# Leaving out the matmuls whose results nobody reads, in a two-block transformer kernel on one core

## The chip, the cores and the metric

One Trainium2 chip, one of its cores. TensorE (PE) multiplies, VectorE (DVE) and ScalarE (ACT) do the elementwise work and empty PSUM, GpSimd (POOL) has a small part, and SyncE (SP) issues most of the DMAs. The metric is the device time in microseconds of one execution, the median over the runs. Lower is better.

## What is computed

The reference runs one sequence of 512 latent tokens and 256 context tokens, width 1024, float32, through three layers. The first has windowed attention with 16 query heads and 4 key heads and a learned sink; a block of 128 latent queries sees its neighbour blocks and all 256 context keys, a context block sees the context alone:

```python
    q_lat, k_lat, v_lat = project(h_lat)
    q_ctx, k_ctx, v_ctx = project(h_ctx)
    ...
        s_lat = jnp.einsum('bqhgd,bkhd->bhgqk', q, k).astype(jnp.float32)
        s_lat = jnp.where(ok, s_lat, NEG_INF)
        s_ctx = jnp.einsum('bqhgd,bkhd->bhgqk', q, k_ctx).astype(jnp.float32)
        p = softmax_with_sink(jnp.concatenate([s_lat, s_ctx], axis=-1), sink_g).astype(v.dtype)
```

The second layer has a gated linear scan (4 heads, both directions, chunks of 64 tokens), of which only the 512 latent rows go on:

```python
        A = jnp.where(lower, jnp.einsum('bqhd,bkhd->bhqk', q_dec, k_inv), 0.0)
        o = jnp.einsum('bhqk,bkhv->bqhv', A, vc) + jnp.einsum('bqhd,bhdv->bqhv', q_dec, S)
        ...
        S = jnp.exp(b_last)[..., None] * S + jnp.einsum('bkhd,bkhv->bhdv', k_end, vc)
```

Each has a multilayer perceptron behind it. The third layer has another attention, a state space model and a mixture of 16 experts. The result is x, 512 by 1024.

## The kernel before, in words

All engines run their own straight program, written by hand in `backbone_kernel`, and meet at semaphores; nothing reorders it. Weights come as tiles of 128 by 1024 on one queue into a ring of 4 (`RAW`), and ScalarE and VectorE split each into a high and a low part (`WH`, `WL`), so that a float32 product becomes three matmuls (`three`, L396 to L398).

**First attention.** The list `heads_of_blocks` gives 96 steps `aa`: 4 key heads g, in each 6 blocks b of 128 queries (0 to 3 latent, 4 and 5 context), in each 4 query heads hh. A step handles 128 queries against 512 keys (b of 0 and 3), 640 keys (b of 1 and 2) or 256 keys (b of 4 and 5). TensorE's part of one step is, in this order: the transposes of the step's exponentials (`transposes`, L734; each transpose is two records in the trace); then `keep_clock`; then the scores two steps ahead (`scores`, L715 to L722 against latent keys, L396 to L398 against context keys); then the weighted values of the step before (`weighted_values`, L745 to L749). At hh of 1 the output of the block before is turned (`out_turned`, L758). ScalarE takes the exponentials (L1177) and the high parts of the transposes (L1186), VectorE the low parts (L1685), the row maxima (L1671, L1675), the scaling of a block's outputs (L1693 to L1706) and, in 64 of the steps, one piece of a modulation product (`mod_stream`, L456).

**Gated scan.** For each of 4 heads h: two tiles of projections, two gate products, a token-major projection of the values (`token_tiles`), then `keep_clock`, then for each direction d the key transposes (`key_transposes`, L844) and `scan`. `scan` alternates per pair of chunks the mixing matrix (L859), the state updates (`updates`, L873, on 64 rows) and, for the four latent pairs, `output` (L889 and L893), which calls `keep_clock` after its waits. Behind a head come two tiles of the output gate (L396 to L398).

`keep_clock` (L447) issues n plain matmuls of 512 columns on 128 rows, with weights and data taken from `HH`, into a PSUM stretch that the following work overwrites with its own first matmul. It has no wait of its own and signals nobody. Its three counts are set at L312:

```python
            for _ in range(n):
                pe.matmul(out, HH[:, KT - 1, 0:P], HH[:, KT - 1, P:P + 512], start=True, stop=True)
```

Of the kernel before, what the change touches and what calls it, by code (L numbers as in the profile page):

```python
# [182 lines left out]
def backbone_kernel(nc, a, out_d):  # L183
# [3 lines left out]
    with ctx:  # L187
# [121 lines left out]
        TWO_PI = 6.283185  # L309
        SSM_PREP = 28  # L310

        STEP_FILL, SCAN_FILL, HEAD_FILL = 1, 2, 12  # L312
        MN = TQ
        SCAN_TILES = [[4, 5, 0, 1, 2, 3], [5, 4, 3, 2, 1, 0]]

# [2070 lines left out]
```

## Time and profile before

| | us |
|---|---|
| median of 3 runs | 3479.77 |
| the three runs | 3477.26, 3479.77, 3495.88 |
| span of the profiled execution | 3475.3 |
| lowest run minus that span | 2.0 |
| mean granted TensorE clock over the span | 0.891 of full |
| first attention, from its first transpose to its end | 216.4 to 586 |
| the four key heads of it begin at | 216.4, 303.1, 411.4, 504.9 |
| gated scan, four heads | 1361.6 to 1749 |

The profile lists only the span of the profiled execution, from its first to its last instruction; its own time in the way of the runs isn't given apart, so the lowest run stands beside it. Busy time, the granted clock and the waits are read from that one execution. In the clock column 1.00 is the upper of TensorE's two levels (2.4 GHz) and 0.50 the lower (1.2 GHz); a value between is a mean over a stretch that has both.

### The profile page before, as it was taken

Reading aid. Unit: us, or ns where it says so; the run is one execution under the profiler, and the core shown is the slowest. Engines: PE = TensorE matmul, PEld = TensorE weight load, DVE = VectorE, ACT = ScalarE, POOL = GpSimd, SP = SyncE. Lnnn points to the kernel's source line nnn. Section 1 sums busy time; section 2 is a strip of 40 time slices with the busy share of each in tenths; the row PEclk is TensorE's granted clock in tenths of the full one; section 3 lists DMA queues with packets and bytes.
Section 4 is the critical chain, followed back from the end, with each engine's and each line's share of the span. In section 5 each row is a group of like instructions: output and inputs, shape, how many; then the busy total and the mean of one; then the engine's idle time right before and its main releaser. Section 6 shows DMA issues by size and latency. Waiting matters only on the chain.

```text
span 3475.3 us, 38477 instructions
## 1 busy us (share of the span) xinstructions
PE 3052.2 (88%) x14418; PEld 2523.9 (73%) x14418; DVE 1751.9 (50%) x2824; ACT 1081.9 (31%) x1673; POOL 172.2 (5%) x151
## 2 busy tenths in 40 slices
PE   1999999879999979888987999887767697999999
PEld 0988887779999957777765888564444376888887
DVE  8456776264654654434425444423388853444433
ACT  2332333331221232322234222334343222222222
POOL 0000000000000000000000000000165300000000
PEclk6996899989999988877798999977687897999999
DMA  5111111123322310100011222111011121222222
GB/s 182 55 37 43 55 54 40 41 78 104 125 105 97 133 43 25 34 33 15 30 59 57 97 96 97 67 49 37 28 49 51 34 89 42 92 96 91 97 91 97
DMA packets 68016, 238.18 MB, mean 69 GB/s; under 512 B 7680, under 2 KB 8192, under 8 KB 67776
## 3 DMA queue, kind: packets, MB, share of 16 engines
q1 hardware_dynamic: 64224, 229.23, 19.7%
q10 hardware_dynamic: 3680, 7.42, 0.7%
q8 instruction: 74, 1.21, 0.2%
q14 instruction: 38, 0.31, 0.0%
HBM read 234.52 MB, written 2.10 MB: 68 GB/s over the span
## 4 chain that ended last, share of the span: by engine, by line
PE 79%; DVE 15%; ACT 3%; issue 2%; POOL 0%; DMA 0%; ACTq 0%; DVEq 0%
PE DP L396 20%; PE DP L398 19%; PE DP L397 19%; PE XP L734 3%; PE XP L1029 2%; DVE PR L2113 2%; PE XP L873 2%; DVE MPROD L456 2%; PE DP L447 1%; DVE TQ L2109 1%; PE XP L509 1%; DVE TQ L536 1%; DVE PR L2103 1%; DVE HL L525 1%; PE DP L893 1%
## 5 line engine op out<-in xcount | busy, mean ns | idle before, releaser
L396 PE MATMUL DP<-HH,WL 128*128 128x512 f32 (+1 forms) x1920 | 745.6, 388 | 129.8 <-DVE WL L389 84.3
L397 PE MATMUL DP<-HH,WH 128*128 128x512 f32 (+1 forms) x1920 | 717.0, 373 | 0.0
L398 PE MATMUL DP<-HL,WH 128*128 128x512 f32 (+1 forms) x1920 | 716.1, 373 | 0.0
L389 DVE TENSOR_TENSOR WL<-RAW,WH 128x1024 fp32r<-128x1024 f32 x327 | 400.5, 1225 | 391.2 <-ACT WH L380 381.4
L396 PEld LDWEIGHTS DP<-HH,WL 128*128 128x128 f32 x1920 | 371.8, 194 | 201.9 <-DVE WL L389 90.3
L396 PE MATMUL DP<-AH,WL 128*128 128x384 f32 (+1 forms) x1296 | 476.8, 368 | 18.5 <-DVE AL L2140 11.1
L380 ACT ACTIVATE WH<-RAW 128x1024 fp32r<-128x1024 f32 x327 | 343.6, 1051 | 467.0 <-PE DP L398 406.3
L398 PE MATMUL DP<-AL,WH 128*128 128x384 f32 (+1 forms) x1296 | 471.8, 364 | 0.0
L397 PE MATMUL DP<-AH,WH 128*128 128x384 f32 (+1 forms) x1296 | 471.6, 364 | 0.0
L397 PEld LDWEIGHTS DP<-HH,WH 128*128 128x128 f32 x1920 | 370.5, 193 | 58.5 <-issue 14.3
L398 PEld LDWEIGHTS DP<-HL,WH 128*128 128x128 f32 x1920 | 369.0, 192 | 47.3
L396 PEld LDWEIGHTS DP<-AH,WL 128*128 128x128 f32 x1296 | 245.2, 189 | 49.2 <-issue 17.2
L397 PEld LDWEIGHTS DP<-AH,WH 128*128 128x128 f32 x1296 | 245.3, 189 | 28.1 <-issue 1.4
L398 PEld LDWEIGHTS DP<-AL,WH 128*128 128x128 f32 x1296 | 245.0, 189 | 26.1
L456 DVE SCALAR_TENSOR_TENSOR MPROD<-RAW,COND 128x1024 f32<-128x1024 f32 x192 | 234.2, 1220 | 6.1 <-DVE MPROD L456 3.8
L509 PE MATMUL XP<-TQ,CONST 128*128 128x384 f32 (+1 forms) x240 | 105.5, 580 | 50.7 <-ACT TQ L503 50.5
L1029 PE MATMUL XP<-PR,TQ 128*128 128x512 f32 x64 | 59.1, 1078 | 76.2 <-DVE PR L2116 76.2
L734 PE MATMUL XP<-CONST,TQ 128*128 128x128 f32 x704 | 112.9, 308 | 6.2 <-DVE HL L1685 5.1
L509 PEld LDWEIGHTS XP<-TQ,CONST 128*128 128x128 f32 x240 | 46.9, 208 | 96.9 <-ACT TQ L503 59.6
L396 PE MATMUL DP<-WH,HL 128*128 128x256 f32 x304 | 94.5, 311 | 23.3 <-issue 23.3
L1177 ACT ACTIVATE TQ<-DP,ST 128x512 f32<-128x512 f32 (+2 forms) x96 | 62.5, 651 | 151.5 <-DVE ST L1675 151.4
L734 PEld LDWEIGHTS XP<-CONST,TQ 128*128 128x128 f32 x704 | 99.8, 217 | 8.0 <-issue 5.3
(319 smaller groups left out, 3899.8 us busy)
## 6 DMA issues: line engine op xcount, KB each, us to landing
RAW<-in_stream SPq DMA_DIRECT2D x423, 512.0 KB, 3.5
MATS<-in_ssm ACTq DMA_DIRECT2D x16, 256.0 KB, 2.6
X<-in_x SPq DMA_DIRECT2D x8, 384.0 KB, 6.9
BW<-in_rel ACTq DMA_DIRECT2D x4, 512.0 KB, 3.6
out<-X SPq DMA_DIRECT2D x8, 256.0 KB, 2.6
COND<-in_cond SPq DMA_DIRECT2D x1, 1024.0 KB, 5.0
CONST<-in_const SPq DMA_DIRECT2D x1, 256.0 KB, 4.9
COS<-in_rope SPq DMA_DIRECT2D x1, 256.0 KB, 11.7
```

The lines of the kernel that those rows point to most:

```text
L380: act.activation(WH[:, nxt.d % WRING, :], RAW[:, nxt.u % RING, :], ACT.Copy).then_inc(hi_done, 1)
L389: dve.tensor_tensor(WL[:, w, :], RAW[:, nxt.u % RING, :], WH[:, w, :].bitcast(F32), ALU.subtract).then_inc(raw_done[nxt.u % RING], 1)
L396: pe.matmul(out, al, bh, start=first, stop=False)
L397: pe.matmul(out, ah, bh, start=False, stop=False)
L398: return pe.matmul(out, ah, bl, start=False, stop=last)
L456: dve.scalar_tensor_tensor(MPROD[:, :], RAW[:, at.u % RING, :], 1.0, COND[:, s, :], ALU.mult, ALU.mult, accum_out=MODT[:, col, s:s + 1]).t ...
L509: last = pe.matmul(XP[:, c, 0:b0 - a0], ONES, TQ[:, k % 2, a0:b0], start=(k == 0), stop=(k == tiles - 1))
L734: last = pe.matmul(XPF[:, to:to + P], PB[:, p, i * P:(i + 1) * P], IDENT, start=True, stop=True)
L873: pe.matmul(XP[:, 2 + c % 2, 0:GLA_DV], KE[rows, m, :], VT[rows, m, :], start=True, stop=True).then_inc(sem("update_made"), 1)
L1029: last = pe.matmul(XP[:, 2 + t % 2, :], CM(k), PR[:, k, :], start=(j == 0 and q == 0), stop=(j == 3 and q == 1))
L1177: act.activation(PB[:, p, 0:n], DPF[:, p * 1024 + 768 - n:p * 1024 + 768], ACT.Exp, bias=ST[:, q, 1, hh:hh + 1], accum_out=ST[:, q, 2, hh: ...
L2113: dve.tensor_tensor(PR[:, k, :], TQ[:, z, 0:LAT], q, ALU.mult).then_inc(sem("ssm_products"), 1)
```

## The change

All three counts become zero, so that `keep_clock` issues nothing at any of its three places. These matmuls wrote 512 columns each that no instruction reads. Everything else is word for word the same.

```diff
-        STEP_FILL, SCAN_FILL, HEAD_FILL = 1, 2, 12
+        STEP_FILL, SCAN_FILL, HEAD_FILL = 0, 0, 0
```

The places where the counts are used (unchanged):

```python
                if aa + 2 < len(work):
                    keep_clock(pe, STEP_FILL, DP[:, 2 * (aa % 2), :])
                    scores(*work[aa + 2])
...
                    keep_clock(pe, SCAN_FILL, DP[:, j % 2, :])
...
                keep_clock(pe, HEAD_FILL, XP[:, 2, :])
```

In the first attention, TensorE's instructions around one step with 512 keys; `TQ` holds the exponentials, `KDH` and `AL` keys and queries (this occurs 94 times):

```order
 L749 MATMUL XP<-VHL,HH 128x128 x3
 L734 MATMUL XP<-CONST,TQ 128x128 x4
-L447 MATMUL DP<-HH 128x512
 L715 MATMUL DP<-KDH,AL 128x384
 L716 MATMUL DP<-KDH,AH 128x384
```

The scores now follow the transposes directly; nothing else moved.

In the scan, TensorE's instructions from the mixing matrix to the first output of a pair of chunks (this occurs 32 times, and takes away two matmuls each time):

```order
 L859 MATMUL DP<-QD,KI 128x128
 L873 MATMUL XP<-VT,KE 128x256 x2
-L447 MATMUL DP<-HH 128x512 x2
 L889 MATMUL DP<-ATM,VT 128x128
 L893 MATMUL DP<-QD,S 128x64 x2
```

The output's matmuls now come straight after the state updates, behind the same waits.

At the start of each of the four heads' scans, between the value projection (`WH` against `HH`) and the key transposes:

```order
 L397 MATMUL DP<-WH,HH 128x256
 L398 MATMUL DP<-WL,HH 128x256
-L447 MATMUL XP<-HH 128x512 x12
 L844 MATMUL XP<-CONST,KEF 128x128 x6
 L873 MATMUL XP<-VT,KE 128x256 x4
```

Between the projection and the key transposes TensorE has nothing left to issue. The other four engines' instructions are the same row for row.

## Rows read from the trace of the kernel before

**Rows 1.** The page: the chain that ended last, shares of the span by engine

```profile
PE 79%; DVE 15%; ACT 3%; issue 2%; POOL 0%; DMA 0%; ACTq 0%; DVEq 0%
```

**Rows 2.** Instructions of L447: whole span, 216 to 590 us, 1360 to 1760 us; ns min/median/max

```profile
L447 PE MATMUL XP<-HH x48: 388/389/398, 1355.3 to 1699.5; 128*128 128x512 f32 x48
...
L447 PE MATMUL DP<-HH x94: 473/480/775, 217.3 to 579.8; 128*128 128x512 f32 x94
...
L447 PE MATMUL DP<-HH x64: 391/628/794, 1369.4 to 1747.3; 128*128 128x512 f32 x64
```

**Rows 3.** Stretches of the first attention: us, PE, PEld, DVE, ACT, POOL busy, clock, DMA

```profile
230.00:277.00 47.00, 46.71 (x322) 39.32 (x321) 36.11 (x75) 18.89 (x42) 0.00 (x0) 1.00 0.15 50
277.90:289.80 11.90, 10.45 (x68) 8.27 (x67) 10.94 (x31) 4.57 (x17) 0.00 (x0) 1.00 0.25 83
...
289.80:347.80 58.00, 58.00 (x213) 47.94 (x213) 28.87 (x66) 14.30 (x35) 0.00 (x0) 0.50 0.09 29
```

**Rows 4.** Stretches, L447 alone: us, PE busy, PEld busy, clock, DMA

```profile
289.80:347.80 58.00, 7.74 (x10) 3.33 (x10) 0.50 0.09 29
...
395.60:426.30 30.70, 5.42 (x7) 2.33 (x7) 0.50 0.16 51
...
494.60:508.20 13.60, 2.32 (x3) 1.00 (x3) 0.50 0.18 56
...
1474.50:1498.10 23.60, 4.86 (x8) 2.04 (x8) 0.50 0.07 23
...
1504.90:1515.20 10.30, 2.44 (x4) 1.00 (x4) 0.50 0.00 0
```

**Rows 5.** Timeline of PE, matmuls of 512 columns in a row, at either clock

```profile
1419.45 0.63 PE L397 MATMUL DP<-HH,WH 128*128 128x512 f32 x1
1419.88 0.63 PE L398 MATMUL DP<-HL,WH 128*128 128x512 f32 x1
...
1423.63 0.39 PE L396 MATMUL DP<-HH,WL 128*128 128x512 f32 x1
1423.86 0.39 PE L397 MATMUL DP<-HH,WH 128*128 128x512 f32 x1
```

**Rows 6.** Timeline of PE: starts of two steps with 640 keys at either clock

```profile
329.26 2.44 PE L734 MATMUL XP<-CONST,TQ 128*128 128x128 f32 x10
331.36 0.77 PE L447 MATMUL DP<-HH 128*128 128x512 f32 x1
...
336.64 1.59 PE L734 MATMUL XP<-CONST,TQ 128*128 128x128 f32 x6
...
432.62 1.33 PE L734 MATMUL XP<-CONST,TQ 128*128 128x128 f32 x10
...
436.70 1.33 PE L734 MATMUL XP<-CONST,TQ 128*128 128x128 f32 x10
```

**Rows 7.** PE's longest kind of wait in the first attention, 216 to 590 us

```profile
PE XP L734 <- DVE HL L1685: 5.1, 11, 0.9
```

**Rows 8.** Stretches, heads 0 and 1 of the scan, each direction; columns as in rows 3

```profile
1361.60:1383.10 21.50, 20.93 (x86) 15.85 (x87) 6.50 (x16) 1.16 (x3) 0.00 (x0) 0.60 0.07 25
1384.90:1404.80 19.90, 18.77 (x86) 14.39 (x86) 7.50 (x19) 0.00 (x1) 0.00 (x0) 0.74 0.00 0
1474.50:1499.00 24.50, 23.97 (x86) 18.25 (x87) 6.57 (x16) 1.15 (x3) 0.00 (x0) 0.52 0.07 22
1500.80:1520.50 19.70, 18.82 (x86) 14.50 (x86) 7.28 (x19) 0.00 (x0) 0.00 (x0) 0.74 0.00 0
```

**Rows 9.** Timeline of PE, head 1: a pair of L447 and the output behind it

```profile
1482.22 1.22 PE L447 MATMUL DP<-HH 128*128 128x512 f32 x2
1483.24 0.63 PE L889 MATMUL DP<-ATM,VT 128*128 128x128 f32 x2
```

**Rows 10.** Timeline of PE: the matmuls ahead of head 0's scan, and the key transposes

```profile
1355.27 2.91 PE L447 MATMUL XP<-HH 128*128 128x512 f32 x12
1359.75 0.88 PE L844 MATMUL XP<-CONST,KEF 128*128 128x128 f32 x6 [1.57 <-ACT VT L1124]
```

## The prediction, made before the changed kernel ran

> **What bounds the kernel now.** I read the chain that ended last first: 79% of it is TensorE [rows 1]. So an instruction taken off TensorE counts wherever TensorE isn't waiting at that place. Then the instructions of L447, the ones that go: 94 in the first attention, 64 in the scan, 48 ahead of the heads' scans [rows 2]. Then the stretches of the first attention, where the reader is to look at PE busy and at the clock column together. Through blocks 0 to 3 PE is busy for 46.71 of 47.00 us at full clock, and DVE for 36.11. In the context blocks (4 and 5) PE is busy for 10.45 of 11.90 us and DVE for 10.94: there VectorE sets the pace. Right behind that the clock is at half for 58.0 us, with PE busy all the time [rows 3]. PE's longest kind of wait in this stage sums to 5.1 us [rows 7]. The scan is alike: PE is busy for 93 to 98% of each direction, at a mean clock of 0.52 to 0.74 [rows 8].
>
> So two things happen when L447 goes. TensorE's queue gets shorter, which is a plain gain. And the clock, which in these two stages goes to and fro, sees another mixture of work. The second can be larger than the first: a step with 640 keys takes 336.64 - 329.26 = 7.4 us at half clock and 436.70 - 432.62 = 4.1 us at full [rows 6]. All else is outside the two stages and stays.
>
> **The change part by part, first with the clock left where it was.** The price of one L447: in a row of 512-column matmuls the next begins 0.43 us later at half clock and 0.23 us later at full [rows 5]. The nearest other row is the pair ahead of a scan output, 1483.24 - 1482.22 = 1.02 us for two at half clock, 0.51 each [rows 9]. The upper end is its own recorded duration, 0.77 us at half (7.74 / 10) [rows 4] and 0.48 at full [rows 2], part of which overlaps its neighbours. I take 0.43 and 0.23 in the attention.
>
> Attention: 10 + 7 + 3 = 20 run at half clock [rows 4]: 20 x 0.43 = 8.6 us. Of the other 74, 21 are in context blocks at full clock (5 in the stretch of rows 3, and 4, 6 and 6 in the other key heads), where VectorE sets the pace, and count nothing; if that cover were gone they'd be worth 21 x 0.23 = 4.8 us. The other 53 give 53 x 0.23 = 12.2 us. Sum -21 us. What is late next there is VectorE, at 77% busy, so it hides little.
>
> Scan: in head 1, 8 + 4 = 12 of 16 run at half clock [rows 4]; head 3 is the same, heads 0 and 2 have 8 each. So 40 at half by 0.51 are 20.4 us, 24 at full by 0.23 are 5.5 us: -26 us.
>
> Ahead of the heads: the last of 12 begins within 3 us of 1355.27, and the key transposes begin at 1359.75 after a wait of 1.57 us for ScalarE's copy [rows 10]. They fill a wait; removing them gives nothing by itself. The same holds in the other heads.
>
> With the clock unchanged the sum is -21 - 26 = -47 us. That is the far end on the fast side.
>
> **What the clock does.** I see from the rows what TensorE did before the clock moved. At full clock it fell behind context blocks with VectorE-bound waits, and behind waits of some us. At half clock it doesn't return merely because PE is busy: 58.0 us with PE busy for 58.00 [rows 3]. It returned after 58.0, 30.7 and 13.6 us [rows 4], in the third step of block 1, the third of block 0 and the first of block 0, each time right behind transposes with their L447. So what PE streams matters and not only whether it's occupied, and L447 is, by its 128 rows and 512 columns, among the densest things in these steps. Without it the return can't come sooner for the same reason, but the transposes stay, and they're the larger dense piece: in the step of rows 6 at half clock they run for some 2.1 us before L447, against its 0.43. So in the attention I expect the return to come about as often as before, and the fall to come some steps sooner in the context blocks. The prices: about 3 more context steps per key head at half. At full clock one takes 11.9 / 5 = 2.4 us, and PE's own work in it is (10.45 - 5 x 0.23) / 5 = 1.9 us [rows 3]; by the ratio of the long steps, (7.4 - 0.43) / (4.1 - 0.23) = 1.8 [rows 5, 6], that would be up to 3.3 us at half, between nothing and 0.9 us more. I take 0.5, since VectorE's pace is then no longer the limit: 4 x 3 x 0.5 = +6 us. Besides there is a chance of under a half that the clock falls at the very beginning, where TensorE waits for the first exponentials, and stays down for two steps at 3 us each: +2 us on average. Attention: -21 + 8 = -13 us.
>
> In the scan L447 is a larger part: 1.02 us ahead of an output of 2.45 us at half clock, and what is left is 64-row updates and 64-column products. The clock returned there only after two to four pairs in every direction (8 at half in the first direction of head 1, 4 in the second [rows 4]). I choose that without them it doesn't return within a direction. Then a direction takes what head 1's first takes at half clock, less its pairs: 24.5 - 4 x 1.02 + 0.7 for its last end at full = 21.1 us. The eight take 169 us; now they take 2 x (21.5 + 19.9 + 24.5 + 19.7) = 171 us [rows 8] (heads 2 and 3 are within some tenths of these), from which I take the 0.5 us of wait behind each second direction, 169 us. Net 0. Then the key transposes run at half where they now run at full, 8 x 0.64 = +5 us (six records of 0.107 more each), and the output gate's tiles behind a head start at half clock instead of full, some 2.7 us of stream at half the pace (an estimate; after the gap behind the scan such a stream still ran at half at 1419.9 and no longer at 1423.6 [rows 5]), 4 x 1.35 = +5 us. Scan: +10 us, between -26 and +15.
>
> **Sum:** -13 + 10 = -3 us.
>
> The Trainium skill, page "TensorE: Matmul & The Clock Gate", section "Loop structure matters more than you think", says that matmuls keep the upper clock while they follow each other and lose it over a long wait. The trace disagrees in part: the clock stayed at half with PE busy for 58.00 of 58.0 us. By that rule alone the attention, which has no long wait, would keep its clock without L447, and the sum would be that of the first rival.
>
> **The rivals.**
> 1. *The clock stays as it is, only the queue shrinks.* For it: L447 is only 0.43 of 7.4 us in a step. Against it: the scan returns to full clock only behind pairs of L447. Time: 3479.8 - 47 = 3433, with VectorE hiding some of it 3440. Chance 0.15.
> 2. *The scan keeps its clock in part, the attention as forecast:* -13 - 10 = -23, 3457. Chance 0.10.
> 3. *The return in the attention comes later (the other side).* Place: blocks 0 to 2 of key heads 1 to 3. A step there costs 7.4 - 0.43 - 3.9 = 3.1 us more at half than at full [rows 5, 6]. Missing the return in blocks 1 and 2 of one key head costs 8 x 3.1 = 25 us, so the kernel is slower by over 0.5% from some 7 more half-clock steps in all, and by 2 key heads +50 us. The far end, half clock from the first fall to the end of the attention, is 3 key heads of an estimated 133 us (8 steps of 7.0, 8 of some 6.3 with 512 keys, 8 context ones of 3.3) against 283 us now from 303.1 to 586: +116 us, 3593. For it: the return took 58 us once with L447. Against: it came in every key head. Time at one key head missed 3502. Chance 0.22.
> 4. *VectorE hides the attention's gain.* It is busy for 77% at full clock, its low parts and maxima alternate with TensorE. Against: PE waits little there. Then +8 + 10 = +18, 3498. Chance 0.10.
> 5. *The forecast,* 3479.8 - 3 = 3476.8, say 3477; its own range 3460 to 3492. Chance 0.43.
>
> That the change doesn't do what it says can't be: the three counts feed the only three calls.
>
> **How the numbers follow.** The sum stands against the profiled span of 3475.3; the lowest run is 2.0 above that and the median 4.5 above, and I apply the difference to the median. Faster by over 0.5% (17 us, about what a measurement of this kernel can tell from no change): rival 1, rival 2 for most of it and a little of the forecast, 0.28. Slower: rival 3 for most, half of rival 4, a little of the forecast, 0.28. Within: 0.44. The range reaches from the slower half of rival 1 to the case of one to two key heads missed, 3438 to 3522.
>
> **What would show it.** In the profile of the changed kernel: L447 is gone; the scan's directions all last about 21 us at a clock of 0.50 (rival 2: some at 0.6 or more and under 19 us); the key transposes run at half; steps with 640 keys take about 3.9 us at full clock, not 4.1 (rival 4: 4.1 still); the attention has three half-clock stretches of 20 to 60 us, which begin inside the context blocks (rival 3: one that reaches through blocks 1 and 2). The prediction would be wrong above all if the clock in the scan still returned, or in the attention no longer did.

## The result, and the profile after

The changed kernel takes 3511.34 us (median of 20 runs, 3508.75 to 3529.64), the kernel before 3485.76 us (20 runs beside them, 3470.83 to 3515.64). The ratio is 1.0075, with a 95% interval of 1.0055 to 1.0094: **slower by 26 us**, where the prediction said 3477 and no measurable change; 3511 lies inside its range of 3438 to 3522. The mean granted clock was 0.861 to 0.867 in each of the 20 runs (median 0.865); in the 76 runs of the kernel before whose clock is listed, beside the experiments, it was 0.880 to 0.900. The profiled execution has a span of 3508.5 us, 33 above that of before.

The bound is the same. From the page of the changed kernel, the chain that ended last, and the clock in 40 slices of the span:

```profile
PE 79%; DVE 15%; ACT 4%; issue 3%; POOL 0%; DMA 0%; ACTq 0%; DVEq 0%
...
PEclk7986778989999997866778999977678897999999
```

For comparison, the two stages as whole stretches in the kernel before (columns as in rows 3). In the attention the clock's mean of 0.86 is 104 of 372 us at half (2 x 0.14 x 372):

```profile
216.40:588.40 372.00, 361.07 (x2112) 299.36 (x2112) 261.07 (x587) 129.68 (x333) 0.00 (x0) 0.86 0.14 46
1359.70:1755.10 395.40, 353.46 (x1697) 289.65 (x1698) 152.08 (x310) 103.81 (x154) 0.00 (x0) 0.79 0.08 26
```

And in the changed kernel: the attention, in it four of its five half-clock stretches and one full-clock stretch; then the scan, and the two directions of head 0:

```profile
214.60:608.30 393.70, 385.54 (x2018) 330.45 (x2018) 261.73 (x588) 131.48 (x333) 0.00 (x0) 0.73 0.13 43
216.00:240.10 24.10, 24.10 (x91) 20.38 (x90) 10.46 (x20) 6.34 (x14) 0.00 (x0) 0.50 0.07 22
240.20:288.20 48.00, 46.57 (x326) 40.29 (x325) 39.21 (x85) 18.99 (x45) 0.00 (x0) 1.00 0.17 56
288.30:360.20 71.90, 71.90 (x272) 61.20 (x272) 39.43 (x88) 19.35 (x50) 0.00 (x0) 0.50 0.11 37
397.00:459.00 62.00, 61.23 (x232) 51.99 (x231) 35.01 (x80) 16.48 (x43) 0.00 (x0) 0.50 0.11 35
496.00:533.00 37.00, 36.87 (x140) 31.47 (x141) 24.49 (x63) 11.41 (x34) 0.00 (x0) 0.50 0.18 57
...
1378.50:1789.70 411.20, 360.87 (x1597) 295.17 (x1598) 152.92 (x310) 103.76 (x154) 0.00 (x0) 0.70 0.07 25
1378.50:1403.00 24.50, 22.93 (x84) 17.59 (x85) 8.13 (x18) 2.89 (x5) 0.00 (x0) 0.50 0.07 22
1403.00:1426.50 23.50, 21.92 (x86) 16.88 (x85) 7.25 (x18) 1.20 (x2) 0.00 (x0) 0.57 0.00 0
```

TensorE has 94 matmuls fewer in the attention (2112 against 2018), and the stage is 21.7 us longer. The half-clock stretches of rows 3 and 4 were 58.0, 30.7 and 13.6 us (a fourth of 10.2 begins at 586.7, behind the last step); now they are 71.9, 62.0, 37.0 and 24 (the last begins in the context blocks of the last key head, with 17 us of it inside the stage), and a new one of 24 us stands at the very start. Half-clock time in the stage went from 104 to 211 us in these two profiles. The scan has 100 matmuls fewer and is 15.8 us longer. The two stages are 37 us; all else came out 4 us shorter.

The queue did shrink as priced. The timeline of the changed kernel gives the starts of one 640-key step at half clock (6.94 us) and one at full (4.06; in the kernel before, the same step took 4.30 with its L447, 354.77 to 359.07):

```profile
333.95 0.95 PE L734 MATMUL XP<-CONST,TQ 128*128 128x128 f32 x3
...
340.89 0.95 PE L734 MATMUL XP<-CONST,TQ 128*128 128x128 f32 x3
...
361.69 0.55 PE L734 MATMUL XP<-CONST,TQ 128*128 128x128 f32 x3
...
365.75 0.44 PE L734 MATMUL XP<-CONST,TQ 128*128 128x128 f32 x2
```

In the scan the clock came back only twice, for 3.4 us each, at the key transposes of the second direction in heads 0 and 3 (hence the 0.57 in the last line above). So most key transposes ran at half (median 421 ns against 273 before), and so did the first tiles behind each head: matmuls in a row still followed at 0.43 us until 1430.97 and at 0.23 us only from 1431.38 on:

```profile
L844 PE MATMUL XP<-CONST,KEF x48: 272/421/477, 1378.5 to 1758.9; 128*128 128x128 f32 x48
```

```profile
1427.39 0.80 PE L396 MATMUL DP<-HH,WL 128*128 128x512 f32 x1 [0.52 <-DVE O L1897]
...
1430.97 0.57 PE L398 MATMUL DP<-HL,WH 128*128 128x512 f32 x1
1431.38 0.39 PE L396 MATMUL DP<-HH,WL 128*128 128x512 f32 x1
```

### The profile page after: what moved, and what is told of

It is laid out like the page before. It is cut to its first block, busy times and chain, and to the rows that moved or that the text cites. A ratio compares the mean times of both kernels' runs of the same rounds, so it can differ in the third digit from the quotient of the medians.

```text
span 3508.5 us, 38068 instructions
## 1 busy us (share of the span) xinstructions
PE 3076.5 (88%) x14212; PEld 2554.2 (73%) x14212; DVE 1753.8 (50%) x2824; ACT 1083.6 (31%) x1673; POOL 172.3 (5%) x151
## 4 chain that ended last, share of the span: by engine, by line
PE 79%; DVE 15%; ACT 4%; issue 3%; POOL 0%; DMA 0%; ACTq 0%; DVEq 0%
PE DP L396 20%; PE DP L397 19%; PE DP L398 19%; PE XP L734 3%; PE XP L873 2%; DVE PR L2113 2%; PE XP L1029 2%; PE XP L509 2%; DVE TQ L2109 1%; DVE MPROD L456 1%; PE DP L893 1%; DVE TQ L536 1%; PE XP L747 1%; DVE PR L2103 1%; DVE HL L525 1%
## 5 line engine op out<-in xcount | busy, mean ns | idle before, releaser
L396 PEld LDWEIGHTS DP<-AH,WL 128*128 128x128 f32 x1296 | 245.2, 189 | 49.2 <-issue 17.1
L734 PE MATMUL XP<-CONST,TQ 128*128 128x128 f32 x704 | 131.0, 342 | 4.7 <-DVE HL L1685 3.6
L734 PEld LDWEIGHTS XP<-CONST,TQ 128*128 128x128 f32 x704 | 116.7, 248 | 6.5 <-issue 4.9
```

The source lines that it names most:

```text
L396: pe.matmul(out, al, bh, start=first, stop=False)
L734: last = pe.matmul(XPF[:, to:to + P], PB[:, p, i * P:(i + 1) * P], IDENT, start=True, stop=True)
```

## The experiments

**The theory after the result:** an L447 is cheap (0.23 or 0.43 us) and, as dense work (matmuls that follow each other without a pause), buys clock that is worth more. **Rivals:** (a) occupancy alone holds the clock, so what the matmul fills doesn't matter; (b) where an L447 stands doesn't matter, only how many there are; (c) the slowdown is one stage's, and the other removals are free; (d) the difference is the scatter of the clock between executions. Below, time at half is worked out from a stretch's clock column: 2 x (1 - clock) x length.

### One count at a time

```
e1:  STEP_FILL, SCAN_FILL, HEAD_FILL = 0, 2, 12
e2:  STEP_FILL, SCAN_FILL, HEAD_FILL = 1, 0, 12
e3:  STEP_FILL, SCAN_FILL, HEAD_FILL = 1, 2, 0
```

> Only the 94 matmuls of the first attention are left out (counts 0, 2, 12). Theory (the clock): the attention's half-clock stretches lengthen as in the changed kernel, its length from the first transpose to the last turned output goes from 372 us to 385 to 395, the scan's directions stay at 19 to 25 us each; in all 10 to 22 us over the kernel before. Rival (TensorE hands its scores over sooner and VectorE can't follow, so the clock only follows): steps with 640 keys at full clock stay at 4.1 us. If each part only shortened TensorE's queue: 21 us faster.

> Only the 64 matmuls ahead of the scan outputs are left out (counts 1, 0, 12). Theory: all eight directions run at a clock of 0.50, about 21.5 us each from the first update to the last output; with the slower start of the output gate 8 to 16 us over the kernel before; attention unchanged at 372 us give or take 10. Rival (the queue only): 26 us faster.

> Only the 48 matmuls ahead of the heads' scans are left out (counts 1, 2, 0). Theory: they fill a wait, and only the key transposes behind them and the first updates run at half clock in some heads: 0 to 4 us slower. Rival (they carry the clock into the scan): 8 us or more slower, with every first direction longer than in the kernel before.

Measured against the kernel before (3482.14 us, 29 runs): without those of the attention 3500.57 us, ratio 1.0073 (1.0042 to 1.0104); without those of the scan 3502.68, 1.0068 (1.0037 to 1.0099); without those ahead of the heads 3469.67, 0.9979 (0.9948 to 1.0010). The three add up to 1.2%, the whole change is 0.75%, within what these intervals allow. The windows of the attention and the scan, for e1 and then for e2:

```profile
214.80:608.40 393.60, 385.50 (x2017) 330.49 (x2018) 261.42 (x588) 131.34 (x333) 0.00 (x0) 0.73 0.13 43
1378.70:1773.90 395.20, 353.33 (x1696) 289.58 (x1697) 152.03 (x310) 103.71 (x154) 0.00 (x0) 0.79 0.08 26
```

```profile
214.40:606.80 392.40, 383.07 (x2112) 317.92 (x2112) 262.03 (x587) 130.28 (x333) 0.00 (x0) 0.80 0.13 44
1377.80:1782.60 404.80, 362.93 (x1632) 296.67 (x1633) 152.74 (x310) 103.69 (x154) 0.00 (x0) 0.73 0.08 25
```

e1 repeats the changed kernel's attention (393.6 us, clock 0.73, the same five stretches) and has the scan of before. Its 640-key steps at full clock took 4.06 us (median) against 4.29 before, so VectorE followed, and its rival falls. e2's scan is 9.4 us longer than that of before. But its attention, whose code is that of before, took 392.4 us and not 372.0, with three half-clock stretches of 61, 61 and 31 us:

```profile
280.60:341.90 61.30, 61.30 (x223) 50.17 (x222) 32.98 (x77) 15.79 (x42) 0.00 (x0) 0.50 0.10 35
393.30:454.50 61.20, 61.20 (x224) 50.56 (x224) 30.89 (x69) 15.16 (x38) 0.00 (x0) 0.50 0.11 35
502.50:533.00 30.50, 30.50 (x112) 24.72 (x112) 17.61 (x42) 8.53 (x25) 0.00 (x0) 0.50 0.16 52
```

The attention of e3 is the same again (392.4 us), and that of e7 below took 344.7. So four profiles of one attention code gave 344.7 to 392.4 us, and the 21.7 us between the first pair of profiles can't price this stage. What carries the verdict are the medians, with the clock of every run: e1's median clock is 0.8765 against 0.890 in the 29 runs of before. Both stages cost time, which speaks against (c), and (d) falls by the intervals. The windows of e3 for head 0's and head 1's second direction:

```profile
1405.00:1426.00 21.00, 19.42 (x94) 14.99 (x93) 7.07 (x18) 1.19 (x2) 0.00 (x0) 0.76 0.00 0
1518.00:1535.10 17.10, 15.52 (x94) 11.68 (x93) 6.97 (x18) 1.19 (x2) 0.00 (x0) 1.00 0.00 1
```

In heads 1 to 3 the second direction ran wholly at full clock without the twelve matmuls ahead of the first; head 0's first direction took 26.9 us against 23.4. In sum e3's scan is 381.6 us against 395.4, in one profile each, and the median can't tell a gain from none: leaving the twelve out costs nothing that the runs resolve.

### The same matmuls with a part of the array

```
e4:   pe.matmul(out, HH[0:32, KT - 1, 0:P], HH[0:32, KT - 1, P:P + 512], start=True, stop=True)
e12:  pe.matmul(out[0:32], HH[:, KT - 1, 0:32], HH[:, KT - 1, P:P + 512], start=True, stop=True)
e13:  pe.matmul(out[:, 0:P], HH[0:32, KT - 1, 0:P], HH[0:32, KT - 1, P:2 * P], start=True, stop=True)
```

> All counts as in the kernel before (1, 2, 12), but each of these matmuls reads 32 rows of HH instead of 128, so that it takes TensorE as long and works a quarter of the array. Theory 1 (what counts is how much of the array works): the clock behaves as in the changed kernel, at or below it, and the time of the matmuls themselves is paid too: 3511 plus 20 to 47 us, over 3525. Theory 2 (what counts is that TensorE is occupied): as the kernel before, 3486 within 8.

> Every L447 stays where it is in the kernel before and streams the same 512 columns over 128 rows, but with 32 instead of 128 columns of weights, so that it fills 32 partitions of its output. The same fill over 32 rows and 128 columns of weights took 3736.5 us. If what counts for the clock is the rows that a stream goes over, this one works like the full fill: 3470 to 3495 us and an attention with 104 to 156 us at half. If it is the number of cells that multiply, a quarter here as there, the clock is mostly at half as it was over 32 rows: 3600 to 3740 us. If the fill over 32 rows was worse than none for another reason (3736.5 against 3511 us without any), this one lies near the changed kernel or the one before, and the reason is to be sought in what changing the rows between matmuls does.

> Every L447 stays where it is in the kernel before, over 32 rows as in the 3736.5 us run, but streams 128 columns instead of 512. In that run an L447 cost more than over 128 rows: the matmul behind it began 0.72 us later at half clock, not 0.43, and it began 0.35 us after the last transpose, since TensorE empties itself when the rows that it uses change. Two things could have kept the clock at half there: that pause at each L447, or the 0.2 to 0.4 us in which only 32 rows work. Here the pause is the same and the stream a quarter as long. If the pause is what does it, the clock is at half for most of the attention again (over 400 us) and the time is 3650 to 3720 us. If it is the time with few rows at work, the kernel is near the one without any L447, 3500 to 3560 us with some 210 to 260 us at half in the attention. Between these, both count.

Over 32 rows: 3736.5 us, ratio 1.0746 (1.0697 to 1.0794). With 32 columns of weights over all rows: 3463.31 us, 0.9904 (0.9865 to 0.9944). Over 32 rows and a quarter as long: 3673.5 us, 1.0519 (1.0434 to 1.0603). The attention's window in e4, e12 and e13:

```profile
217.20:793.50 576.30, 574.12 (x2111) 465.54 (x2112) 265.93 (x588) 132.99 (x333) 0.00 (x0) 0.52 0.09 30
```

```profile
215.30:590.50 375.20, 365.14 (x2111) 293.59 (x2112) 261.63 (x588) 130.09 (x333) 0.00 (x0) 0.85 0.13 46
```

```profile
217.00:752.30 535.30, 533.12 (x2111) 455.52 (x2112) 265.85 (x588) 132.95 (x333) 0.00 (x0) 0.54 0.10 32
```

PE counts as busy for 574 of 576 us in e4, and the clock is at half for all but 4% of it. So (a) falls: being occupied by this column doesn't hold the clock. Nor is it a matter of how many columns of weights multiply, since e12 does as well as the kernel before or better. How that column misleads shows in the timelines around one L447 at half clock, in e13, then in the kernel before, and at the same place of the changed kernel; each begins with the last transpose record of a step:

```profile
243.98 0.42 PE L734 MATMUL XP<-CONST,TQ 128*128 128x128 f32 x1
244.33 0.47 PE L447 MATMUL DP<-HH 32*128 32x128 f32 x1
244.73 0.69 PE L715 MATMUL DP<-KDH,AL 64*128 64x384 f32 x1
```

```profile
331.28 0.42 PE L734 MATMUL XP<-CONST,TQ 128*128 128x128 f32 x1
331.36 0.77 PE L447 MATMUL DP<-HH 128*128 128x512 f32 x1
332.06 0.69 PE L715 MATMUL DP<-KDH,AL 64*128 64x384 f32 x1
```

```profile
335.97 0.42 PE L734 MATMUL XP<-CONST,TQ 128*128 128x128 f32 x1
336.32 0.69 PE L715 MATMUL DP<-KDH,AL 64*128 64x384 f32 x1
```

128 columns take 0.107 us in a row at half clock (a quarter of the 0.43 of rows 5), yet the score's matmul begins 0.40 us after L447. In e4, with 512 columns, it begins 0.72 us after (and 0.70 in the kernel before; the 0.43 of my expectation is that of like matmuls in a row). In both L447 begins 0.35 us after the transpose ahead, 0.07 in the kernel before, and 0.07 in e12 too. Where the number of rows changes, the next matmul begins about 0.3 us late at half clock, and the busy column counts this pause as work. What makes the pause no run shows. The grouped instructions of L447 in e13 have idle time ahead of them, all of it TensorE's weight loads (PEld) and not its matmuls; in the attention it is 20.1 us ahead of 90 of them, and none in the kernel before:

```profile
  issue: 30.5, 106
```

Set e13 beside the changed kernel: from the last transpose to the score it is 0.75 us and not 0.35, that is 0.29 us more of pause and 0.11 of a stream over 32 rows. The clock goes from 0.73 to 0.54, some 280 us more at half. In the kernel before each step has 0.43 us more than the changed one, all of it dense, and the clock is 0.86 (0.80 to 0.94 in other profiles). That is the theory with both signs. My expectation for e13 asked pause or few rows. A stream four times as long over few rows (e4) took 63 us more, of which some 158 x 0.32 = 50 us are the stream itself, so it changed the clock little (0.54 to 0.52); that leaves the pause, but what few rows alone would do, without a pause, no run separates.

### More of them, and elsewhere

```
e5:   STEP_FILL, SCAN_FILL, HEAD_FILL = 2, 4, 18
e6:  +keep_clock(pe, 4, XP[:, 2, :])                      # ahead of the first transposes
     -keep_clock(pe, STEP_FILL, DP[:, 2 * (aa % 2), :])
     +keep_clock(pe, 0 if near else 3, DP[:, 2 * (aa % 2), :])
e7:   STEP_FILL, SCAN_FILL, HEAD_FILL = 1, 0, 18
     +if c == 2:
     +    keep_clock(pe, 2, DP[:, 3, :])                  # ahead of the wait of an update
      key_transposes(h, d)
     +keep_clock(pe, 4, DP[:, 3, :])
e8:   e6 and e7 together
```

> More of the same: counts 2, 4, 18 in place of 1, 2, 12. Theory (the clock follows how much of the array works): the clock returns sooner in the attention and the scan; the extra 94 + 64 matmuls cost 0.23 each at full clock, 36 us in all, against some 50 us of half-clock loss in the attention and some 30 in the scan that can go: 3445 to 3490, and the attention's half-clock share under a quarter. Rival (the matmuls are mere load, the clock is luck): 3482 + 36 to 60 = 3518 or more.

> First attention only: no such matmuls in steps of latent blocks, 3 in each step of a context block, where TensorE waits for VectorE, and 4 ahead of the first transposes, where it waits for the first exponentials; scan as in the kernel before. Theory: the clock never falls inside the attention, which then lasts 4 x 80 = 320 us in place of 372 to 393; 3425 to 3440 in all. Rival (the clock falls somewhere and can't return without the matmuls in the latent steps): an attention of over 390 us.

> Scan only: none ahead of the outputs, 4 between key transposes and the first update, where TensorE waits for ScalarE's copy, 2 ahead of the third update's wait, 18 in place of 12 ahead of a head; attention as in the kernel before (1). Theory: the directions run at full clock and last 15 us each in place of 21 to 26; the scan goes from 395 to 330 us; 3482 - 60 = 3422 within 15. Rival: the clock falls on the 64-row updates all the same and then can't return within a direction: 24 us each as in the changed kernel, 3500.

> The last two together. Theory: the two gains add, 3482 - 55 - 60 = 3367 within 20, and the spread between executions shrinks to a few us since the clock has no chance left in these stages. Rival: only one of them holds, 3420 to 3440.

| kernel | L447 | us | ratio to before |
|---|---|---|---|
| e5, about twice as many | 388 | 3441.44 | 0.9865 (0.9833 to 0.9896) |
| e6, attention moved into waits | 206 | 3427.48 | 0.9818 (0.9788 to 0.9849) |
| e7, scan moved into waits | 214 | 3424.27 | 0.9802 (0.9757 to 0.9846) |
| e8, both moved | 214 | 3364.16 | 0.9640 (0.9610 to 0.9670) |

Twice as many L447 in the same places (e5) hold the attention at 1.00 as well. The windows of the attention and the scan in e5, in e7 (whose attention is that of the kernel before) and in e8, with head 0's first direction of e8 as a third line:

```profile
216.20:561.60 345.40, 337.71 (x2205) 272.52 (x2206) 260.53 (x587) 129.00 (x333) 0.00 (x0) 1.00 0.15 50
1332.30:1717.80 385.50, 347.63 (x1778) 282.57 (x1779) 151.79 (x310) 103.91 (x154) 0.00 (x0) 0.87 0.08 27
```

```profile
216.20:560.90 344.70, 333.79 (x2112) 276.62 (x2112) 260.47 (x587) 128.91 (x333) 0.00 (x0) 0.94 0.15 50
1332.10:1665.70 333.60, 307.94 (x1699) 251.46 (x1700) 151.04 (x310) 103.73 (x154) 0.00 (x0) 0.94 0.09 31
```

```profile
217.60:538.90 321.30, 314.53 (x2108) 263.80 (x2107) 259.09 (x587) 127.80 (x331) 0.00 (x0) 1.00 0.16 53
1309.00:1642.40 333.40, 307.65 (x1698) 251.25 (x1699) 151.04 (x310) 103.89 (x154) 0.00 (x0) 0.94 0.09 31
1309.00:1324.20 15.20, 15.13 (x91) 11.12 (x92) 7.89 (x18) 2.85 (x5) 0.00 (x0) 1.00 0.11 36
```

Against (b): e8 has 214 L447 where the kernel before has 206, and is 3.6% faster. A direction of the scan takes 15.1 us, at full clock, where it took 21 to 26 with its key transposes. Its attention ran at 1.00, with 2108 matmuls there, about as many as before. Placed where TensorE waits for VectorE or ScalarE, the matmul fills the wait and takes little time of its own: the two context blocks of key head 0 took 21.7 us in e8 (276.13 to 297.87) with three L447 a step, and 20.6 in e7 (277.71 to 298.29) with one, both at full clock, so 1.2 us for 16 L447 whose streams are 3.7. e8's six runs lie within 3.1 us of each other (3362.73 to 3365.78), where the 11 of the kernel before beside them spread over 31 us, and the 20 above over 45. e8 is the version that beats both kernels, by 4.3% against the changed one (0.9640 / 1.0075 = 0.957).

The scatter isn't gone from this placement, though. The four L447 ahead of the first transposes don't secure the start. In e6's profiled execution, the slowest of its seven (3449.69 us against a median of 3427.48), the clock fell ahead of them and stayed at half for 51 us, through steps without L447; in e8's it fell as well, and was back after 3.4 us. The first two lines are e6's, the third e8's:

```profile
214.70:265.90 51.20, 51.20 (x191) 43.76 (x190) 21.86 (x43) 13.19 (x29) 0.00 (x0) 0.50 0.06 21
266.00:343.00 77.00, 76.14 (x509) 63.49 (x507) 64.39 (x148) 30.68 (x81) 0.00 (x0) 1.00 0.18 56
...
214.90:218.30 3.40, 3.40 (x11) 2.79 (x12) 1.57 (x4) 1.56 (x4) 0.00 (x0) 0.50 0.00 0
```

### Which places in the attention

```
e9:  +keep_clock(pe, 0 if near else 1, DP[:, 2 * (aa % 2), :])   # for the STEP_FILL line
e10:  STEP_FILL, SCAN_FILL, HEAD_FILL = 0, 0, 0
     +keep_clock(pe, 4, XP[:, 2, :])                      # ahead of the first transposes
```

> In the first attention L447 runs only in the context blocks, one in each step (24 steps, less the last two), and not in the steps with 640 and 512 keys; the scan is as in the kernel before. What the attention's clock depends on is what I ask. If the dense work that holds the clock is needed where TensorE waits for VectorE, that is in the context blocks, the attention keeps or betters the half-clock part of the kernel before (104 us in its profile, 155.6 in the same code's attention in another run), and the time is 3455 to 3485 us. If each L447 counts alike wherever it stands, most of them are gone and the attention does as in the changed kernel: 211 us at half, a fall at 216, and 3490 to 3505 us.

> The changed kernel, with four L447 put back at one place: ahead of the first transposes of the attention, where TensorE waits for the first exponentials. If that wait is what costs the clock at the very beginning (half from 216 to 240 us in the changed kernel), that stretch goes, worth 5 steps' difference or some 10 us, and nothing else changes: 3500 us against 3511, the later half-clock stretches of 36 to 72 us stay. If the clock's first fall also sets when the later ones come, the stretches behind it shift and the gain is anything between 0 and 30 us. If those four do nothing the profile shows 216 to 240 at half again and 3511 us.

e9: 3465.64 us, 0.9925 (0.9896 to 0.9955). e10: 3501.92 us, 1.0031 (1.0001 to 1.0060). Both beside a kernel before of 3495.89. The attention's windows, e9 and then e10:

```profile
216.30:575.80 359.50, 348.23 (x2047) 294.79 (x2048) 260.31 (x587) 129.87 (x333) 0.00 (x0) 0.85 0.14 48
```

```profile
216.20:589.60 373.40, 365.89 (x2019) 313.69 (x2018) 261.60 (x588) 131.42 (x333) 0.00 (x0) 0.78 0.13 46
```

The 30 L447 of the context blocks (32 steps less the last two, and not 22, as my expectation counted) alone hold the clock about as well as all 94 did (0.85 against 0.80 to 0.94 in the profiles of before's code), and the 64 others took more time than they gave. They may not be idle: e9's clock fell at the start, as the changed kernel's did, and in none of the six profiles with an L447 of 128 rows in every step (before, e2, e3, e5, e7, e12) did it fall there. With four L447 at the start e10's first steps ran at full clock: from the first transposes to the second step of block 1 it takes 17.1 us (216.24 to 233.32) against 27.5 in the changed kernel (214.63 to 242.11). The first fall is gone, and the stretch behind the first context blocks is 48 us long instead of 72; whether the second follows from the first, one profile doesn't tell. Nor are the four L447 shown to be the cause: in e6 and e8 the clock fell with the same four in place. By the two ratios, 1.0031 against 1.0075, they are worth about 15 us, with an uncertainty nearly as large.

## Why the prediction was wrong

**What bounds it, and the price of L447: right.** 0.44 us off a 640-key step at half clock (7.38 to 6.94) and 0.24 at full (4.30 to 4.06), as taken; VectorE hid none of it there. In context steps at full clock it hid nearly all (median 2.32 us before, 2.29 after), as forecast.

**The attention, -21 + 8 = -13 us: wrong, and this is the step that failed.** The -21 of the queue was right as far as the steps show it; the +8 for the clock was some +40. It rested on "the return to come about as often as before", because the transposes are "the larger dense piece", and on few and cheap half-clock steps in the context blocks. By the medians, leaving out the 94 matmuls alone (e1) cost 18 us (25 by the ratio, 15 to 36 by its interval) instead of giving 13. The clocks of the runs say why: 0.8765 in e1 against 0.890 is 2 x (0.1235 x 3501 - 0.110 x 3482) = 99 us more at half, of which 1 - 4.06 / 6.94 = 0.41 is loss, 40 us; less 21 of queue, +19. (The first pair of profiles gives 107 us more at half and +23, but that it comes so near to its +21.7 is in part luck, since the kernel before took anything from 345 to 392 us there.)

Where the time went, in the profiles: context steps at half took 3.2 us (median), 0.9 above those at full, the upper end of what I allowed and not the 0.5 taken, and there were 22 of them against 8 in the profile of before. The changed kernel, e1 and e10 all lost the clock in the context blocks of the last key head too, where no profile with L447 in the context steps did. The return came in each key head, 13.9, 31.3 and 23.4 us later than in the profile of before. That looks like rival 3 in a milder form, but the returns in key heads 2 and 3 came in the same steps in e2 and e3, which have all 94; so that lateness isn't shown to be L447's. Where I wrote of "PE busy for 58.00 of 58.0 us" I had a column that counts as work the pauses at each change between 128 and 64 rows (0.28 us at the one behind L447). I had compared L447 with the transposes by length, and e13 shows how much less than that matters: 0.29 us more of pause and 0.11 of a stream over few rows, in steps of some 7 us, took the clock from 0.73 to 0.54.

**The fall at the start, "under a half", +2 us:** it came in the changed kernel, in e1 and in e9, lasted 24 us and not two steps, and cost 10.4 us (27.5 us in the changed kernel, 17.1 in e10).

**The scan, net 0 + 5 + 5 = +10 us: right in mechanism, measured +15.8.** The clock returned only for 3.4 us in two heads. The eight directions with their key transposes (first transpose to the end of the last output) sum to 193.8 us against 184.0, +9.8 where +5 was forecast; the tiles behind a head ran at half for 4.0 us (1427.39 to 1431.38), and the stretch up to L927 took 1.3 to 2.7 us more per head, +7.8 in all where +5 was forecast. The work between the heads came out 1.8 us shorter.

**The twelve ahead of a head, nothing by themselves: right as far as the runs resolve it** (e3, 0.9948 to 1.0010).

**The Trainium skill's rule** (page "TensorE: Matmul & The Clock Gate", section "Loop structure matters more than you think") asks for matmuls that follow each other back to back. The fills inside waits (e6 to e8) agree with it in direction, though the section's bad case is a long wait at each matmul, and the waits filled here were of 1 us and less, and of 4.3 us ahead of a head (the changed kernel's wait for ScalarE's copy before the key transposes of head 0). As I applied it, by the busy column, it would have given the first rival's 3433 us, and the run says 3511.

**The baseline:** the profiled execution that the sum was read from, 3475.3 us, was one of the quicker ones of a kernel that spreads over 45 us; the same attention code took 345 us (e7) to 392 us (e2) in other profiles. A sum of -3 us on one profile had an error of tens of us in it, which the range covered and the point didn't say. That 3511 fell inside the range is owed to this width and not to the mechanism.

## What to carry to other kernels

Where the granted clock goes to and fro, price a TensorE instruction twice: what it takes of the queue, and what it does to the time at half clock. A dense matmul that nobody reads is worth most inside a wait, where it costs little (1.2 us for 16 in e8); between other matmuls it may hold the clock at a price or only cost it. Look at starts, not at the busy column, to see whether TensorE pauses. And where executions of one kernel differ by tens of us, take the clock of many runs and not one profile to price a stage.

## What the runs showed of the hardware

- A change in the number of rows that a matmul uses costs about 0.3 us at half clock: 0.35 us from a transpose record to a 32-row matmul, 0.07 to a 128-row one. A change of the output columns from 128 to 32 doesn't (0.07, e12). The profile's busy column hides the pause (574.12 of 576.30 us).
- 0.29 us of such pause and 0.11 of a stream over 32 rows, in each step of some 7 us, brought the attention's clock from 0.73 to 0.54, and 0.43 us of dense work to between 0.80 and 0.94, in different executions of one code.
- Matmuls that fill 32 output partitions over all 128 rows held the clock as well as full ones (0.9904).
- The kernel's run-to-run scatter goes with the clock: over 29 runs of the kernel before the quickest (3449.57 us) had a granted clock of 0.900 and the slowest (3515.61) one of 0.880. e8's six runs, at 0.920 to 0.922, lie within 3.1 us.
